# Paged attention with its score rows standing twice on the partitions

## The chip, the cores and the metric

One core of one Trainium2 chip runs the whole program in one launch. The metric is the device time of one execution in microseconds (us). Three runs of the kernel before gave 2151.07, 2154.58 and 2155.91 us, a median of 2154.58 us.

## The reference

One layer of a decoder is computed for a prompt (1 x 1024 tokens) and for samples (8 sequences of 8 new tokens), with the same weights. The change touches only the attention of the samples, which have 2048 cached tokens each, kept in pages of 128:

```
past_c  = cache_kv_latent[l][page_table].reshape(8, 2048, 256)
past_pe = cache_k_rope[l][page_table].reshape(8, 2048, 32)
c_keys  = concatenate([past_c, c_new]);  pe_keys = concatenate([past_pe, pe_new])
s  = (einsum('bqhl,btl->bhqt', q_lat, c_keys) + einsum('bqhr,btr->bhqt', q_pe, pe_keys)) * ATTN_SCALE
s  = where(query position >= key position, s, -1e30)
pr = softmax(s)                                   # float32, 8 heads x 8 queries = 64 rows, 2048 + 8 keys
o  = einsum('bhqt,btl->bqhl', pr, c_keys)
```

The convolution group of the same layer, a causal depthwise convolution of width 31 over 4 x 128 channels, also matters: its taps run on VectorE inside this stage.

## The kernel before, in words

The program is a row of stages, each with one instruction stream per engine, written out by hand with counting semaphores; no scheduler moves anything. The stage here is `paged_attention_stage`; a stage begins when all engines have left the one ahead. It takes the 8 sequences b = 0 to 7 one after the other (a loop over six of them, two written out behind it).

For one sequence the 64 rows R (8 heads x 8 queries) stand on partitions 0 to 63. GpSimd gathers the pages (`gather_pages`, two indirect DMAs, 2 MB and 256 KB, into one of two buffers); for sequence b+2 it waits on `attended` of sequence b, since that frees the buffer. TensorE runs, in this order for step b:

- `turn(b+1)`: 36 transposes of gathered tiles in nine groups q = 0 to 8, through two PSUM banks in turn. ScalarE copies groups 0, 1, 2, 7 and 8 out (`ACT_GROUPS`), VectorE 3 to 6 (`DVE_GROUPS`, L1354); group q waits until group q-2 is copied.
- `attend(b)`: when `exped` says that the exponentials are there, 16 transposes of the probabilities (L1245) and one of the new tokens' (L1249); when they have been copied to SBUF (L1343, L1404), 16 products with the gathered latents (L1255, 64 columns loaded, 256 streamed) and one with the new tokens (L1257).
- `score(b+1)`: for each of four blocks of 512 keys one product with the rope keys (L1223) and two with the latents (L1225), 64 columns loaded and 512 streamed; then three for the 64 new tokens (L1228, L1230). Behind the second block stands `turn_out(b)` (L1263), which transposes the output and waits on `normed`, VectorE's scaled output.

VectorE, for each step: mask on the new tokens' scores (L1385), maximum over 2048 scores (L1387) and over the new (L1389), their joint maximum times the scale (L1391); the four copies of `turn`; sum and reciprocal (L1396, L1398); copies of the turned probabilities (L1403, L1404); then about twelve taps of the convolution, each one instruction on 128 x 1024 (L378) and one on 128 x 64 (L381), split 5:4:2 by the scaling of the output (L1408) and the copy of the turned output (L1412). ScalarE stages the queries of b+1 (L1310, L1312), copies, and takes the exponentials (L1334, L1336).

A float32 product is one instruction of the program and two records in the trace; a transpose is one record.

Of the kernel before, what the change touches and what calls it, by code (L numbers as in the profile page):

```python
# [18 lines left out]
P = 128  # L19
# [1053 lines left out]
def paged_attention_stage(nc, K):  # L1073


    with ExitStack() as ctx:
# [13 lines left out]
        def taps_at(b, part):  # L1090
# [12 lines left out]
        prob = sb("prob", [R, PAST + SAMPLE])  # L1103
        prob_t = sb("prob_t", [P, PER_ROW * R])
        prob_new = sb("prob_new", [SAMPLE, R])
        o = sb("o", [R, KV_LORA])
        tops, sums = sb("tops", [R, 3]), sb("sums", [R, 4])
# [15 lines left out]
            sem(x) for x in ("new_masked", "tops_found", "top_ready", "exped", "summed", "inv_ready"))  # L1123
        probs_turned, act_probs, dve_probs, attended, normed, o_turned, o_copied, may_go = (
# [3 lines left out]
        scores = K.ps[0:R, 0:BANK, :].rearrange("p a b -> p (a b)")  # L1128
        prob_banks = [K.ps[:, 6, :], K.ps[:, 5, :]]
        last = K.ps[:, 7, :]  # L1130
        o_acc, s_new = last[0:R, 0:KV_LORA], last[0:R, 256:256 + SAMPLE]
# [6 lines left out]
        def token(position):  # L1138


            own, j = divmod(position, BANK)
            return j * BANK + own
# [28 lines left out]
        def _(pe):  # L1171
# [44 lines left out]
            def score(b, between=None):  # L1216

                copied(b, GROUPS)
                copied(b, GROUPS - 2)
                pe.wait_ge(staged, 2 * b + 2)  # L1220
                for c in range(BANK):
                    at = slice(c * 512, (c + 1) * 512)
                    nc.tensor.matmul(scores[:, at], q_rope[:, c * R:(c + 1) * R], rope_t[:, :], start=True, stop=False)  # L1223
                    for l in range(KC):
                        nc.tensor.matmul(scores[:, at], q_lat[:, l, :], lat_t[:, l, at], start=False, stop=l == KC - 1)  # L1225
                    if c == 1 and between is not None:
                        between()
                nc.tensor.matmul(s_new, q_rope[:, 2 * R:3 * R], new_rope_t[:, :], start=True, stop=False)  # L1228
                for l in range(KC):
                    mm = nc.tensor.matmul(s_new, q_lat[:, l, :], K.c[:, l, SEQ:T], start=False, stop=l == KC - 1)  # L1230
                mm.then_inc(scored, 1)

            def attend(b, s, more):
                pe.wait_ge(exped, 2 * b + 2)
                if more:

                    copied(b + 1, GROUPS - 1)

                pe.wait_ge(o_copied, KC * b)

                pe.sem_inc(may_go, 1)
                for h in range(2):
                    for j in range(PER_ROW // 2):
                        t = h * (PER_ROW // 2) + j
                        mm = nc.tensor.transpose(prob_banks[h][:, j * R:(j + 1) * R], prob[:, t * P:(t + 1) * P],  # L1245
                                                 K.ident[0:R, 0:R])
                    if h == 0:
                        mm.then_inc(probs_turned, 1)
                nc.tensor.transpose(new_turn, prob[:, PAST:], K.ident[0:R, 0:R]).then_inc(probs_turned, 1)  # L1249
# [7 lines left out]
                nc.tensor.matmul(o_acc, prob_new[:, :], new_rows[:, :], start=False, stop=True).then_inc(attended, 1)  # L1257

            def turn_out(b):
                pe.wait_ge(normed, b + 1)  # L1260
                pe.sem_inc(may_go, 1)
                for l in range(KC):
                    mm = nc.tensor.transpose(o_turn[:, l * R:(l + 1) * R], o[:, l * P:(l + 1) * P],  # L1263
                                             K.ident[0:R, 0:R])
                mm.then_inc(o_turned, 1)
# [8 lines left out]
            pe.wait_ge(prepared, 5)  # L1274
            pe.wait_ge(lat_out, 2)
# [19 lines left out]
        def _(act):  # L1295
# [10 lines left out]
            def stage(b):  # L1306

                if not isinstance(b, int) or b > 0:
                    act.wait_ge(scored, b)
# [17 lines left out]
            def step(b, s, more):  # L1327
                if more:
                    stage(b + 1)
                    copies(b + 1, ACT_GROUPS[0:3])  # L1330
                act.wait_ge(top_ready, b + 1)
# [4 lines left out]
                nc.scalar.activation(prob[:, PAST:], s_new, ACT.Exp, bias=tops[:, 2:3], scale=SCALE,  # L1336
                                     accum_out=sums[:, 1:2]).then_inc(exped, 1)
# [4 lines left out]
                act.wait_ge(attended, b)  # L1342
# [5 lines left out]
        def _(dve):  # L1348
            def copies(b):
                if b > 0:  # L1350
                    dve.wait_ge(scored, b)
# [6 lines left out]
            nc.vector.memset(new_rope_t[:, :], 0.0).then_inc(prepared, 1)  # L1358
            dve.wait_ge(rows_turned, 1)
# [23 lines left out]
            def step(b, s, more):  # L1383
                dve.wait_ge(scored, b + 1)
# [4 lines left out]
                nc.vector.tensor_reduce(tops[:, 1:2], s_new, AX_X, ALU.max).then_inc(tops_found, 1)  # L1389
                dve.wait_ge(tops_found, 2 * b + 2)  # L1390
                nc.vector.tensor_scalar(tops[:, 2:3], tops[:, 0:1], tops[:, 1:2], -SCALE, ALU.max, ALU.mult  # L1391
                                        ).then_inc(top_ready, 1)
                if more:
                    copies(b + 1)
                dve.wait_ge(exped, 2 * b + 2)
                nc.vector.tensor_tensor(sums[:, 2:3], sums[:, 0:1], sums[:, 1:2], ALU.add).then_inc(summed, 1)  # L1396
                dve.wait_ge(summed, b + 1)
                nc.vector.reciprocal(sums[:, 3:4], sums[:, 2:3]).then_inc(inv_ready, 1)  # L1398
                dve.wait_ge(probs_turned, 2 * b + 2)

                if b > 0:
                    dve.wait_ge(attended, b)
# [3 lines left out]
                dve.wait_ge(inv_ready, b + 1)  # L1406
                dve.wait_ge(attended, b + 1)
                nc.vector.tensor_scalar(o[:, :], o_acc, sums[:, 3:4], None, ALU.mult).then_inc(normed, 1)  # L1408
# [1344 lines left out]
```

## Time and profile before

| | |
|---|---|
| median of three runs | 2154.58 us |
| the profiled execution | 2156.27 us |
| its span, first to last instruction | 2154.40 us |
| busy, of the span: TensorE (PE) / VectorE (DVE) / ScalarE (ACT) / GpSimd (POOL) | 90% / 56% / 22% / 24% |
| paged stage: first score product / last tap | 221.99 us / 448.19 us |
| in it, from the first mask (235.75) to the last (425.11): 189.36 us, busy PE / DVE | 178.37 / 164.36 us |

Busy time of an engine is the union of its records. PEld is the loading of weights, which runs beside PE. Matmul records overlap, so the distance of two starts, and not the length of a record, is what one costs in a stream. The granted clock of TensorE is 1.00 at 2.4 GHz and 0.50 at 1.2 GHz.

### The profile page before, as it was taken

The page shows a single profiled execution, that of the slowest core. Times are in us where ns is not written, and L with a number is a line of the kernel's source. Part 1 is how long each engine was busy: PE and PEld are TensorE (multiplying, and loading weights), DVE is VectorE, ACT ScalarE, POOL GpSimd, SP SyncE. Part 2 cuts the span into 40 slices and gives each one's busy share as a digit, 9 for nine tenths or more (in the row PEclk, how much of TensorE's full clock was granted, in tenths as well). Part 3 has the DMA queues.
Part 4 walks back from the last instruction along what each step waited for, and adds up shares of the span by engine and source line. Part 5 has one row for each costly group of instructions (what it writes and reads, how often), then busy time and mean ns, then how long its engine had stood idle before and what let it go on. Part 6 is the DMA issues. An engine that isn't in the chain of part 4 may idle for free. (4 is left out here: it accounts for less than half of the span.)

```text
span 2154.4 us, 27922 instructions
## 1 busy us (share of the span) xinstructions
PE 1941.5 (90%) x10946; PEld 1696.6 (79%) x10946; DVE 1195.8 (56%) x1720; ACT 479.4 (22%) x789; POOL 517.5 (24%) x277
## 2 busy tenths in 40 slices
PE   6998999889999898799948979999999999999985
PEld 6997444445667897689827968999999999999984
DVE  7785588856756437723313578454445445444537
ACT  4021222124444523212212233001001101100011
POOL 3330011010000127821003532322322323223220
PEclk9999999989999999899979989999999999999997
DMA  5215222110000213400072211111111111111102
GB/s 161 84 40 86 88 88 88 44 59 1 1 1 1 90 41 110 146 33 18 0 285 99 77 52 40 40 49 39 39 49 39 41 46 39 49 39 39 49 14 83
DMA packets 42712, 128.37 MB, mean 60 GB/s; under 512 B 12464, under 2 KB 18736, under 8 KB 40016
## 3 DMA queue, kind: packets, MB, share of 16 engines
q1 hardware_dynamic: 40128, 105.72, 14.7%
q0 software_dynamic: 1792, 18.88, 2.3%
q10 hardware_dynamic: 720, 2.79, 0.4%
q8 instruction: 49, 0.80, 0.2%
q14 instruction: 23, 0.19, 0.0%
HBM read 118.81 MB, written 8.56 MB: 59 GB/s over the span
## 5 line engine op out<-in xcount | busy, mean ns | idle before, releaser
L252 POOL CAST w_hi<-raw 128x1024 fp32r<-128x1024 f32 x114 | 136.2, 1195 | 1184.6 <-PE ps L281 621.2
L281 PE MATMUL ps<-xo_hi,w_hi 128*128 128x384 f32 (+1 forms) x1248 | 295.3, 335 | 36.9 <-DVE xo L2458 16.3
L254 POOL TENSOR_TENSOR w_lo<-raw,w_hi 128x1024 fp32r<-128x1024 f32 x114 | 300.8, 2638 | 9.1
L281 PE MATMUL ps<-xo_lo,w_hi 128*128 128x384 f32 (+1 forms) x1248 | 291.5, 331 | 0.0
L281 PE MATMUL ps<-xo_hi,w_lo 128*128 128x384 f32 (+1 forms) x1248 | 291.0, 331 | 0.0
L281 PEld LDWEIGHTS ps<-xo_hi,w_hi 128*128 128x128 f32 x1248 | 219.3, 190 | 43.8 <-issue 35.9
L281 PEld LDWEIGHTS ps<-xo_lo,w_hi 128*128 128x128 f32 x1248 | 219.7, 190 | 0.2
L281 PEld LDWEIGHTS ps<-xo_hi,w_lo 128*128 128x128 f32 x1248 | 219.1, 190 | 0.0
L2413 DVE TENSOR_TENSOR ffn_g_prompt<-ffn_g_prompt,ffn_rstd 128x1024 f32<-128x1024 f32 x22 | 67.8, 3082 | 208.8 <-ACT ffn_g_sample L2293 208.8
L2458 DVE TENSOR_TENSOR xo<-ps,xo 128x768 f32<-128x768 f32 (+1 forms) x160 | 108.4, 719 | 134.1 <-PE ps L281 134.1
L378 DVE SCALAR_TENSOR_TENSOR x<-u_prompt,vecs,x 128x1024 f32<-128x1024 f32 x120 | 163.1, 1359 | 0.0
L281 PE MATMUL ps<-ffn_hid_hi,w_hi 128*128 128x384 f32 (+2 forms) x528 | 130.3, 345 | 8.4 <-DVE ffn_hid_lo L2450 4.8
L281 PE MATMUL ps<-ffn_hid_lo,w_hi 128*128 128x384 f32 (+2 forms) x528 | 123.6, 332 | 0.0
L281 PE MATMUL ps<-ffn_hid_hi,w_lo 128*128 128x384 f32 (+2 forms) x528 | 122.8, 331 | 0.0
L281 PE MATMUL ps<-hx_hi,w_hi 128*128 128x384 f32 (+1 forms) x384 | 90.8, 345 | 14.9 <-PEq L1429 8.4
L281 PEld LDWEIGHTS ps<-ffn_hid_hi,w_hi 128*128 128x128 f32 x528 | 91.7, 191 | 14.8 <-issue 8.8
L281 PEld LDWEIGHTS ps<-ffn_hid_lo,w_hi 128*128 128x128 f32 x528 | 92.4, 191 | 3.4 <-issue 3.0
L871 PEld LDWEIGHTS ps<-v,mla_prob_t 128*128 128x128 f32 x576 | 72.7, 191 | 27.8 <-issue 23.4
L281 PEld LDWEIGHTS ps<-ffn_hid_hi,w_lo 128*128 128x128 f32 x528 | 92.1, 191 | 0.7
L281 PE MATMUL ps<-h_hi,w_hi 128*128 128x384 f32 x336 | 77.1, 338 | 17.1 <-DVE h_lo L614 17.1
L2302 ACT ACTIVATE ffn_hid_hi<-ffn_hid 128x1088 fp32r<-128x1088 f32 x22 | 24.5, 1112 | 294.3 <-PE ps L281 259.2
L281 PE MATMUL ps<-hx_lo,w_hi 128*128 128x384 f32 (+1 forms) x384 | 86.2, 333 | 0.0
(326 smaller groups left out, 3281.9 us busy)
## 6 DMA issues: line engine op xcount, KB each, us to landing
raw<-in_units SPq DMA_DIRECT2D x128, 512.0 KB, 3.2
xs_keys<-in_cache_k_t SPq DMA_DIRECT2D x8, 1024.0 KB, 10.0
xs_vals<-in_cache_v_t SPq DMA_DIRECT2D x16, 512.0 KB, 12.7
x<-in_x_t SPq DMA_DIRECT2D x8, 544.0 KB, 9.0
out_y_t<-x SPq DMA_DIRECT2D x2, 1792.0 KB, 6.6
out_old<-in_x_t ACTq DMA_DIRECT2D x5, 544.0 KB, 3.7
out_old<-in_x_t SPq DMA_DIRECT2D x3, 544.0 KB, 7.0
mla_wq<-in_w_q_t SPq DMA_DIRECT2D x1, 1536.0 KB, 9.0
```

The source lines that it names most:

```text
L252: nc.gpsimd.tensor_copy(K.w_hi[:, s, :], K.raw[:, s, :]).then_inc(K.hi_done[s], 1)
L254: nc.gpsimd.tensor_tensor(K.w_lo[:, s, :], K.raw[:, s, :], K.w_hi[:, s, :].bitcast(F32), ALU.subtract).then_inc(K.split_done[s], 1)
L281: mm = nc.tensor.matmul(out(at, n), w, x(k, at, n), start=first and k == 0 and p == 0, stop=last and k == len(tiles) - 1 and p == 2)
L378: nc.vector.scalar_tensor_tensor(cv, u, scale, cv, ALU.mult, ALU.add).then_inc(tapped, 1)
L871: mm = nc.tensor.matmul(o_acc, prob_t[:, n % 2 * QT + j, :], K.v[:, j, h, :], start=j == 0, stop=j == i)
L2302: nc.scalar.activation(hid_hi[:, slot, :], hid[:, :], ACT.Identity).then_inc(hid_hi_made, 1)
L2413: nc.vector.tensor_tensor(g_p, g_p, rstd[:, 0:SEQ], ALU.mult).then_inc(g_scaled, 1)
L2458: ins = nc.vector.tensor_tensor(y_at, acc, y_at, ALU.add)
```

## The change

The 64 rows stand twice on the partitions: partitions 0 to 63 (`LOWER`) hold the first 1024 keys of the past, 64 to 127 (`UPPER`) the second. Score blocks c and c+2 go to the two halves of the same PSUM bank, and their products alternate; the same for the 16 products of L1255, of which t goes to the lower and t+8 to the upper half of `o_acc`. The past's scores are then 128 x 1024, and maximum, exponential and the copy of the output work on 128 partitions. VectorE joins the two halves' maxima and sums by copies from one half to the other. The probabilities take eight transposes of 128 x 128 in place of sixteen of 64 x 128. The two halves of the output are added in `turn_out`, which becomes a product with `fold` (two identities above one another, made once). `turn_out` now stands behind the first pair of blocks. `scored`, `attended`, `top_ready`, `inv_ready`, `tops_found` and `summed` count more steps each; two semaphores are added, one of them not used.

```diff
-        scores = K.ps[0:R, 0:BANK, :].rearrange("p a b -> p (a b)")
+        LOWER, UPPER = slice(0, R), slice(R, 2 * R)
+        scores = K.ps[:, 0:BANK // 2, :].rearrange("p a b -> p (a b)")
...
-                    pool.wait_ge(attended, b - 1)
+                    pool.wait_ge(attended, 2 * b - 2)
...
-                for c in range(BANK):
-                    at = slice(c * 512, (c + 1) * 512)
-                    nc.tensor.matmul(scores[:, at], q_rope[:, c * R:(c + 1) * R], rope_t[:, :], start=True, stop=False)
+                for c in range(BANK // 2):
+                    halves = [(rows, c + BANK // 2 * n) for n, rows in enumerate((LOWER, UPPER))]
+                    for rows, d in halves:
+                        nc.tensor.matmul(K.ps[rows, c, :], q_rope[:, d * R:(d + 1) * R], rope_t[:, :], start=True,
+                                         stop=False)
                     for l in range(KC):
-                        nc.tensor.matmul(scores[:, at], q_lat[:, l, :], lat_t[:, l, at], start=False, stop=l == KC - 1)
-                    if c == 1 and between is not None:
+                        for rows, d in halves:
+                            mm = nc.tensor.matmul(K.ps[rows, c, :], q_lat[:, l, :], lat_t[:, l, d * 512:(d + 1) * 512],
+                                                  start=False, stop=l == KC - 1)
+                    if c == 0 and between is not None:
                         between()
+                mm.then_inc(scored, 1)
...
-                for t in range(PER_ROW):
-                    if t == PER_ROW // 2:
+                for t in range(2 * BANK):
+                    if t == BANK:
                         pe.wait_ge(dve_probs, b + 1)
-                    at = token(t) * KV_LORA
-                    nc.tensor.matmul(o_acc, prob_t[:, t * R:(t + 1) * R], past[s][:, at:at + KV_LORA], start=t == 0,
-                                     stop=False)
+                    for n, rows in enumerate((LOWER, UPPER)):
+                        at = token(t + 2 * BANK * n) * KV_LORA
+                        mm = nc.tensor.matmul(o_acc[rows], prob_t[:, t * P + n * R:t * P + (n + 1) * R],
+                                              past[s][:, at:at + KV_LORA], start=t == 0, stop=n == 1 and t == 2 * BANK - 1)
+                mm.then_inc(attended, 1)
...
-                    mm = nc.tensor.transpose(o_turn[:, l * R:(l + 1) * R], o[:, l * P:(l + 1) * P],
-                                             K.ident[0:R, 0:R])
+                    mm = nc.tensor.matmul(o_turn[:, l * R:(l + 1) * R], o[:, l * P:(l + 1) * P], fold[:, :],
+                                          start=True, stop=True)
...
-                nc.scalar.activation(prob[:, 0:PAST], scores, ACT.Exp, bias=tops[:, 2:3], scale=SCALE,
+                nc.scalar.activation(prob[:, :], scores, ACT.Exp, bias=tops[:, 3:4], scale=SCALE,
                                      accum_out=sums[:, 0:1]).then_inc(exped, 1)
...
+            nc.vector.tensor_tensor(fold[:, :], K.ident[:, 0:R], K.ident[:, R:2 * R], ALU.add).then_inc(folded, 1)
...
                 nc.vector.tensor_reduce(tops[:, 0:1], scores, AX_X, ALU.max).then_inc(tops_found, 1)
...
+                nc.vector.tensor_copy(tops[LOWER, 2:3], tops[UPPER, 0:1]).then_inc(tops_found, 1)
+                dve.wait_ge(tops_found, 4 * b + 3)
+                nc.vector.tensor_tensor(tops[LOWER, 2:3], tops[LOWER, 2:3], tops[LOWER, 1:2], ALU.max
+                                        ).then_inc(tops_found, 1)
...
+                dve.wait_ge(top_ready, 2 * b + 1)
+                nc.vector.tensor_copy(tops[UPPER, 3:4], tops[LOWER, 3:4]).then_inc(top_ready, 1)
...
-                nc.vector.tensor_scalar(o[:, :], o_acc, sums[:, 3:4], None, ALU.mult).then_inc(normed, 1)
+                nc.vector.tensor_scalar(o[:, :], o_acc, sums[:, 4:5], None, ALU.mult).then_inc(normed, 1)
```

On TensorE, from the transposed probabilities of one sequence to `turn_out` in the score of the next, before (`paged_prob` are the probabilities, `paged_prob_t` their transposes, `x` a buffer of gathered latents, `v` the transposed latents):

```order
L1245 MATMUL ps<-ident,paged_prob 128x64 x16
L1249 MATMUL ps<-ident,paged_prob 64x64
L1255 MATMUL ps<-x,paged_prob_t 64x256 x16
L1257 MATMUL ps<-paged_new_rows,paged_prob_new 64x256
L1174 REGISTER_ALU
L1220 ISA
L1223 MATMUL ps<-paged_rope_t,paged_q_rope 64x512
L1225 MATMUL ps<-v,paged_q_lat 64x512 x2
L1223 MATMUL ps<-paged_rope_t,paged_q_rope 64x512
L1225 MATMUL ps<-v,paged_q_lat 64x512 x2
L1263 MATMUL ps<-ident,paged_o 128x64 x2
```

and the same place now:

```order
L1259 MATMUL ps<-ident,paged_prob 128x128 x8
L1263 MATMUL ps<-ident,paged_prob_tail 64x64
L1270 MATMUL ps<-x,paged_prob_t 64x256 x16
L1273 MATMUL ps<-paged_new_rows,paged_prob_new 64x256
L1182 REGISTER_ALU
L1228 ISA
L1232 MATMUL ps<-paged_rope_t,paged_q_rope 64x512 x2
L1236 MATMUL ps<-v,paged_q_lat 64x512 x4
L1279 MATMUL ps<-paged_fold,paged_o 128x64 x2
```

The number of score and output products and their shapes stay; their order changes, so that neighbours write different halves of the partitions, and eight transposes go. `turn_out` stands behind the same number of products, and has become a product.

On VectorE, from the maximum over the scores to the reciprocal of the sum, before (`paged_tops` holds maxima, `paged_sums` sums; `v<-ps` are the four copies of `turn`):

```order
L1387 TENSOR_REDUCE paged_tops<-ps 64x1
L1389 TENSOR_REDUCE paged_tops<-ps 64x1
L1391 TENSOR_SCALAR paged_tops<-paged_tops 64x1
L1354 COPY v<-ps 128x2x256 x4
L1396 TENSOR_TENSOR paged_sums<-paged_sums 64x1
L1398 RECIPROCAL paged_sums<-paged_sums 64x1
```

and now:

```order
L1405 TENSOR_REDUCE paged_tops<-ps 128x1
L1407 TENSOR_REDUCE paged_tops<-ps 64x1
L1409 COPY paged_tops<-paged_tops 64x1
L1411 TENSOR_TENSOR paged_tops<-paged_tops 64x1
L1414 TENSOR_SCALAR paged_tops<-paged_tops 64x1
L1417 COPY paged_tops<-paged_tops 64x1
L1371 COPY v<-ps 128x2x256 x4
L1421 COPY paged_sums<-paged_sums 64x1
L1423 TENSOR_TENSOR paged_sums<-paged_sums 64x1
L1425 TENSOR_TENSOR paged_sums<-paged_sums 64x1
L1427 RECIPROCAL paged_sums<-paged_sums 64x1
L1429 COPY paged_sums<-paged_sums 64x1
```

Three one-column instructions are added ahead of the four copies and three behind them.

## Rows read from the trace of the kernel before

**Rows 1.** Windows: length, busy us (records) of PE, PEld, DVE, ACT, POOL, clock, DMA.

```profile
222.00:227.65 5.65, 5.65 (x7) 1.63 (x8) 0.00 (x0) 0.00 (x0) 0.58 (x1) 0.50 0.97 376
227.65:235.75 8.10, 8.10 (x26) 2.88 (x25) 0.00 (x1) 0.00 (x0) 0.00 (x0) 1.00 0.07 29
263.36:289.97 26.61, 25.46 (x120) 13.20 (x121) 23.70 (x40) 6.32 (x12) 3.41 (x2) 1.00 0.23 89
289.97:317.65 27.68, 25.55 (x120) 13.19 (x121) 23.49 (x39) 7.49 (x13) 3.41 (x2) 1.00 0.23 85
425.11:429.05 3.94, 0.00 (x0) 0.00 (x0) 2.75 (x4) 1.12 (x1) 0.00 (x0) 1.00 0.00 0
429.05:435.88 6.83, 5.46 (x26) 3.75 (x27) 3.69 (x8) 1.82 (x5) 0.00 (x0) 0.50 0.00 0
```

**Rows 2.** Timeline, sequence 1: start, length, engine, line, what, [idle before, releaser].

```profile
263.37 0.22 DVE L1385 TENSOR_TENSOR ps<-ps,paged_mask 64x64 f32<-64x64 f32 x1 [2.05 <-PE ps L1230]
...
265.94 0.20 DVE L1391 TENSOR_SCALAR paged_tops<-paged_tops 64x1 f32<-64x1 f32 x1
...
266.07 2.71 DVE L1354 COPY v<-ps 128x512 f32<-128x512 f32 x4
...
270.94 0.22 DVE L1403 COPY paged_prob_new<-ps 64x64 f32<-64x64 f32 x1 [1.91 <-PE ps L1249]
...
278.66 1.07 PE L1223 MATMUL ps<-paged_rope_t,paged_q_rope 128*64 128x512 f32 x2
278.84 0.47 DVE L1408 TENSOR_SCALAR paged_o<-ps,paged_sums 64x256 f32<-64x256 f32 x1
...
287.70 1.88 PE L1225 MATMUL ps<-v,paged_q_lat 128*64 128x512 f32 x4
...
289.97 0.23 DVE L1385 TENSOR_TENSOR ps<-ps,paged_mask 64x64 f32<-64x64 f32 x1 [0.65 <-PE ps L1230]
290.04 1.28 ACT L1310 ACT_TABLE_LOAD   x1 [19.06 <-PE ps L1230]
...
293.74 2.92 DVE L1354 COPY v<-ps 128x512 f32<-128x512 f32 x4 [0.98 <-PE ps L1213]
```

**Rows 3.** Groups of instructions in the paged stage: busy us, mean ns, idle before.

```profile
L1225 PE MATMUL ps<-v,paged_q_lat 128*64 128x512 f32 x128 | 61.9, 607 | 0.0
L1255 PE MATMUL ps<-paged_past,paged_prob_t 128*64 128x256 f32 x128 | 30.2, 396 | 0.4
L1387 DVE TENSOR_REDUCE paged_tops<-ps 64x1 f32<-64x2048 f32 x8 | 18.2, 2273 | 0.0
L1334 ACT ACTIVATE paged_prob<-ps,paged_tops 64x2048 f32<-64x2048 f32 x8 | 15.7, 1960 | 23.2 <-DVE paged_tops L1391 23.2
```

**Rows 4.** Timeline of TensorE in the sample cross-attention stage, four 32-row outputs alternating.

```profile
1137.44 3.64 PE L1962 MATMUL ps<-xs_vals,xs_prob_t 128*32 128x512 f32 x32 [0.52 <-DVE xs_prob_t L2017]
```

**Rows 5.** Timeline of the last gather DMAs of sequences 1 and 2, and their median landing.

```profile
221.63 0.95 POOL L688 DMA_INDIRECT past_rope<-in_cache_pe,page_rows  x1 [0.30 <-issue]
...
252.40 2.33 POOL L688 DMA_INDIRECT x<-in_cache_c,page_rows  x1 [29.82 <-PE ps L1257]
...
255.03 1.09 POOL L688 DMA_INDIRECT past_rope<-in_cache_pe,page_rows  x1 [0.30 <-issue]
...
past_rope<-in_cache_pe,page_rows POOLq DMA_INDIRECT x7, 7.8
```

**Rows 6.** Weight loads of eight transposes, at the half clock and at the full.

```profile
203.19 1.57 PEld L1213 LDWEIGHTS ps<-ident,x 128*128 128x128 f32 x8 [0.23 <-ACT paged_rope_t L1300]
...
264.61 0.91 PEld L1213 LDWEIGHTS ps<-ident,x 128*128 128x128 f32 x8 [0.49 <-ACT paged_rope_t L1300]
```

**Rows 7.** Timeline of TensorE in the last sequence.

```profile
430.42 1.94 PE L1245 MATMUL ps<-ident,paged_prob 64*128 64x64 f32 x16 [5.35 <-ACT paged_prob L1336]
...
432.39 8.82 PE L1255 MATMUL ps<-paged_past,paged_prob_t 128*64 128x256 f32 x32
...
441.14 0.64 PE L1257 MATMUL ps<-paged_new_rows,paged_prob_new 64*64 64x256 f32 x2
```

More of the change, by code:

```diff
@@ L1102, in paged_attention_stage @@
         mask = sb("mask", [R, DEC_B * SAMPLE])
-        prob = sb("prob", [R, PAST + SAMPLE])
+        prob = sb("prob", [P, PAST // 2])
+        prob_tail = sb("prob_tail", [R, SAMPLE])
         prob_t = sb("prob_t", [P, PER_ROW * R])
         prob_new = sb("prob_new", [SAMPLE, R])
-        o = sb("o", [R, KV_LORA])
-        tops, sums = sb("tops", [R, 3]), sb("sums", [R, 4])
+        o = sb("o", [P, KV_LORA])
+        fold = sb("fold", [P, R])
+        tops, sums = sb("tops", [P, 4]), sb("sums", [P, 5])
         qlat = sb("qlat", [P, KC * DEC_B, R])[:, :, :].rearrange("p (l b) r -> p l b r", l=KC)
@@ L1127, in paged_attention_stage @@
         block = ctx.enter_context(nc.Block())
-        scores = K.ps[0:R, 0:BANK, :].rearrange("p a b -> p (a b)")
+        LOWER, UPPER = slice(0, R), slice(R, 2 * R)
+        scores = K.ps[:, 0:BANK // 2, :].rearrange("p a b -> p (a b)")
         prob_banks = [K.ps[:, 6, :], K.ps[:, 5, :]]
         last = K.ps[:, 7, :]
-        o_acc, s_new = last[0:R, 0:KV_LORA], last[0:R, 256:256 + SAMPLE]
+        o_acc, s_new = last[:, 0:KV_LORA], last[LOWER, 256:256 + SAMPLE]
         new_turn, o_turn = K.ps[0:SAMPLE, 0, 0:R], K.ps[:, 6, 0:KC * R]
@@ L1242, in attend @@
                 for h in range(2):
-                    for j in range(PER_ROW // 2):
-                        t = h * (PER_ROW // 2) + j
-                        mm = nc.tensor.transpose(prob_banks[h][:, j * R:(j + 1) * R], prob[:, t * P:(t + 1) * P],
-                                                 K.ident[0:R, 0:R])
+                    for j in range(BANK):
+                        t = h * BANK + j
+                        mm = nc.tensor.transpose(prob_banks[h][:, j * P:(j + 1) * P], prob[:, t * P:(t + 1) * P],
+                                                 K.ident[:, :])
                     if h == 0:
                         mm.then_inc(probs_turned, 1)
-                nc.tensor.transpose(new_turn, prob[:, PAST:], K.ident[0:R, 0:R]).then_inc(probs_turned, 1)
+                nc.tensor.transpose(new_turn, prob_tail[:, :], K.ident[0:R, 0:R]).then_inc(probs_turned, 1)
                 pe.wait_ge(act_probs, b + 1)
-                for t in range(PER_ROW):
-                    if t == PER_ROW // 2:
+                for t in range(2 * BANK):
+                    if t == BANK:
                         pe.wait_ge(dve_probs, b + 1)
-                    at = token(t) * KV_LORA
-                    nc.tensor.matmul(o_acc, prob_t[:, t * R:(t + 1) * R], past[s][:, at:at + KV_LORA], start=t == 0,
-                                     stop=False)
-                nc.tensor.matmul(o_acc, prob_new[:, :], new_rows[:, :], start=False, stop=True).then_inc(attended, 1)
+                    for n, rows in enumerate((LOWER, UPPER)):
[3 more added lines that the diff above has]
+                mm.then_inc(attended, 1)
+                nc.tensor.matmul(o_acc[LOWER], prob_new[:, :], new_rows[:, :], start=False, stop=True).then_inc(attended, 1)
             def turn_out(b):
@@ L1274, in _ @@
             pe.wait_ge(prepared, 5)
+            pe.wait_ge(folded, 1)
             pe.wait_ge(lat_out, 2)
@@ L1308, in stage @@
                 if not isinstance(b, int) or b > 0:
-                    act.wait_ge(scored, b)
+                    act.wait_ge(scored, 2 * b)
                 nc.scalar.activation(q_lat[:, :, :], qlat[:, :, bass.ds(b, 1), :].rearrange("p l a r -> p l (a r)"),
@@ L1350, in copies @@
                 if b > 0:
-                    dve.wait_ge(scored, b)
+                    dve.wait_ge(scored, 2 * b)
                 for q in DVE_GROUPS:
@@ L1383, in step @@
             def step(b, s, more):
-                dve.wait_ge(scored, b + 1)
+                dve.wait_ge(scored, 2 * b + 2)
                 nc.vector.tensor_tensor(s_new, s_new, mask[:, b * SAMPLE:(b + 1) * SAMPLE], ALU.add
```

35 lines of the change are left out of this document (21 added, 14 removed).

## The prediction

> **What bounds the kernel now.** I read the page first (TensorE busy 90% of the span, VectorE 56%), then the windows of the paged stage, since a share over the span says nothing of one stage, then the timeline of one sequence there. The windows make both engines look like the bound: in sequence 1, of 26.61 us TensorE is busy 25.46 and VectorE 23.70 [rows 1]. The timeline says how they stand to each other. The reader is to see three points of VectorE: the mask at 263.37, L1403 at 270.94, the next mask at 289.97 [rows 2]. Between the first two VectorE waits for TensorE's transposes (1.91 us at L1403). Behind L1403 it has copies and taps that wait for nothing, until 289.97 - 0.65 = 289.32: 18.4 us. Beside these TensorE does its output and score products, 270.94 to 289.97: 19.0 us. So the part of TensorE that the change shortens runs beside 18.4 us of VectorE which it does not shorten, and VectorE waits only 0.65 us for it (2.05 us in the first sequence, the wait at 263.37).
>
> **TensorE's products.** In a stream of 512 columns a record costs 0.43 us: four take 1.88, less the last one's length of about 0.6, over three [rows 2, 3]. A score over the past has 12 products, 24 records, 10.3 us; the 32 output records fill 278.66 - 270.94 less 0.7 for L1257 and the start, 7.0 us [rows 2]. No row of before has two 64-row halves alternating. The nearest is the sample cross attention, where four 32-row outputs alternate: 32 records of 512 columns in 3.64 us, against 32 x 0.43 = 13.8 one after the other [rows 4]. They run almost four beside one another, at the same spacing. Bounds: nothing gained (each alone) to half the time; I take half, 5.2 us of the score and 3.5 of the output, 8.7 a sequence, some 70 us of TensorE's time in eight. Eight big transposes for sixteen small ones I cost at nothing (twice the columns, half the number), between 0.5 us gained and lost, and `fold` at 0.1 us of TensorE, hidden by its own new slack; without that slack they would be in full on the path. The Trainium skill, "TensorEngine Tiling (Array Packing)", "Tiling Modes", says that changing the tiling mode drains TensorE. No row shows the price here; taking the length of a record over its spacing, 0.16 us, three times a sequence, it would be 0.5 us of the same slack and 0.5 us of the sum at the end.
>
> **VectorE, sequences 1 to 6.** Four of their steps take 26.6 us and two, where ScalarE loads a table ahead of its copies, 27.68 (one of each in [rows 1]): 161.8 us. Now: the maximum reads half as many scores per partition, 2.27 us [rows 3] becomes 1.2; three one-column steps come ahead of the copies, 0.20 to 0.24 each as L1391 [rows 2], +0.7. The three behind the copies fall into the 1.9 us at L1403 and cost nothing; with that wait gone they would cost 0.7. With the 0.65 gone, a step is 26.6 - 0.65 - 1.1 + 0.7 = 25.6 us at TensorE's full clock. In the other two the copies start 293.74 - 289.97 = 3.8 us behind the mask instead of 2.7; `scored` will now come before the mask, so that the table load (1.28 us [rows 2]) is over in time, and these too are 25.6. Gain: 161.8 - 6 x 25.6 = 8.2 us.
>
> **What is late next.** Count from L1403. The output products end at +4.3, and only then may the next gather start. It takes 0.3 + 2.6 us of issue and 7.8 to land, 10.7 in all (252.40 to 255.03 and on [rows 5]): +15.0. The score's first half is done at +7.0, waits for the scaled output (278.84 + 0.47 - 270.94 = +8.4 [rows 2]) and ends at +12.5. So the gather, hidden today behind 11 us of score, will hold TensorE from +12.5 to +15.0; then three groups of `turn` go through, and TensorE waits again for VectorE's first copy, which stands behind its taps and maximum: +18.4 + 2.6 + 0.7 = +21.7. None of this delays VectorE, but TensorE now idles about 10 us of 25.6 in pieces of 2 to 4 us. After 3.94 us without a record its clock was 0.50 for 6.83 us, 5.46 of them busy [rows 1]. I expect that fall in most steps, just before groups 5 to 8 of `turn` and the transposes of the probabilities, and these are on VectorE's path. Weight loads of eight transposes take 1.57 us at half clock and 0.91 at full [rows 6], 0.08 us a record; 25 records are 2.1 us, of which the copies between groups hide a part. Bounds 0 and 2.1 a step; I take 1.2, or 7.2 us in six, so that 1.0 us of the 8.2 is left. The Trainium skill, "TensorE: Matmul & The Clock Gate", "HAM oscillation", says that bursts between waits run at half clock, which is against this change; by it alone the price would be the full 2.1 a step.
>
> **Head.** The first score runs from 222.00 to the mask at 235.75 with nothing else to do, 5.65 us of it at half clock [rows 1]. Twelve pairs and one of stagger: 6.6 at 0.86 us in these 5.65, 6.4 at 0.43 = 2.8, then 0.65 for the new tokens: 9.1 instead of 13.75. Gain 4.65. The gather of sequence 1 has landed at 221.63 + 7.8 = 229.4 [rows 5], before 231.1. The wait of 2.05 us behind it, in the first step, goes as well.
>
> **Tail.** In the last sequence nothing stands beside: maximum -0.4, exponential (1.96 us [rows 3] to about 1.1) -0.9. From the first transpose to the end of L1257 is 430.42 to 441.78, 11.4 us [rows 7]. With 5.46 us at half clock as before: nine transposes 2.0, eight pairs at 0.43, eight at 0.22, 0.65: 7.8. At half clock throughout 10.2. Gain 4.9, at least 2.5; I take 4.4.
>
> **Sum.** 4.65 + 2.05 + 1.0 + 4.4 = 12.1 us off the profiled execution's 2156.27, 2144.2; the median of the runs stands 1.7 below that execution, so 2142.5. With every bound at its worse end 4.65 + 2.05 + 8.2 - 12.6 + 2.5 = 4.8 off, 2149.8.
>
> **Rivals.**
> (a) The clock holds, or its fall lies in VectorE's shadow: 4.65 + 2.05 + 8.2 + 4.9 = 19.8 off, 2134.8. For it: in the step with the table load TensorE has 27.68 - 25.55 = 2.1 us without a record, and the clock stays at 1.00 [rows 1]. Against: the new waits are longer and come twice a step. 20%.
> (b) The halves do not run beside each other, and the change does not do what it says: 64-row outputs are no 32-row ones. Then 19.0 us beside 18.4 stay, and the rest is within 2 us: 2154.5. Against it [rows 4]. 10%.
> (c) Slower: the half clock lasts through output and score. Output 16 x 0.43 + 1.4 = 8.3, score 12 x 0.86 + 1.9 = 12.2, together 20.5 us: past VectorE's 18.4, from where TensorE decides again, and its transposes follow at half clock, 7.6 + 2.1 = 9.7. Six steps of 30.2 and twice 1.1 for the table load are 183.4, +21.6; +1 in the first step, less 4.65 and 2.5: 15.5 slower, 2170. For it: a clock lost anew each 25 us. Against: it came back after 5.65 us of products at 227.65 and after 5.46 at 435.88 [rows 1], and here some 10 us follow without a pause. 10%.
>
> **Chances.** The forecast 60%, 2136 to 2150. About 0.2%, 4.3 us, is what a measurement tells from no change. Faster: the forecast but for 5 of its 60, and (a): 0.75. Same: those 5 and (b): 0.15. Slower: (c), 0.10. The range from 2133 to 2153 leaves out (c) and the outer part of (a) and (b).
>
> **What the new profile would show.** Right: two records of the score starting within some 0.05 us or overlapping by whole lengths, 24 in about 5.5 us; the mask without a wait for TensorE from sequence 1 on, masks 26 to 27.5 us apart in all steps alike; TensorE idle ahead of the first transposes of each sequence and again ahead of group 5, clock 0.50 at these; the first mask near 231. Wrong: masks 25.6 apart with a clock of 1.00 (a); score records 0.43 apart one by one (b); masks that wait for the score, which runs at 0.86 a pair (c). A VectorE step behind L1403 much over 18.4 us would break the sum in a way that I have not costed.

## The result and the profile after

| | us, median (range, runs) | of the kernel before, ratio [95%] |
|---|---|---|
| before | 2155.39 (2151.07 to 2155.91, 5) | |
| changed | 2145.1 (2138.83 to 2146.33, 5) | 0.9948 [0.9937, 0.9959] |
| changed, once more in the experiments | 2145.57 (2133.01 to 2146.8, 6) | 0.9939 [0.992, 0.9958] |

Faster by 10 us, where 12 were forecast. The profiled execution of the first row took 2138.83 us (span 2137.0), the lowest of its five; that of the second 2146.8 (span 2145.0), the highest of its six and 1.2 above their median. Below, "the first" and "the second" are these two executions; most lines shown are of the first, and the account uses both.

One sequence in the first (timeline from the mask of sequence 1 to that of sequence 2; columns as in [rows 2]):

```profile
252.89 0.22 DVE L1403 TENSOR_TENSOR ps<-ps,paged_mask 64x64 f32<-64x64 f32 x1
253.03 1.21 DVE L1405 TENSOR_REDUCE paged_tops<-ps 128x1 f32<-128x1024 f32 x1
...
255.01 0.15 DVE L1417 COPY paged_tops<-paged_tops 64x1 f32<-64x1 f32 x1
255.19 1.29 DVE L1371 COPY v<-ps 128x512 f32<-128x512 f32 x2
...
255.93 1.25 PE L1221 MATMUL ps<-ident,x 128*128 128x128 f32 x8 [1.86 <-DVE v L1371]
...
258.81 1.06 PE L1259 MATMUL ps<-ident,paged_prob 128*128 128x128 f32 x8 [0.18 <-ACT v L1319]
...
260.08 0.22 DVE L1434 COPY paged_prob_new<-ps 64x64 f32<-64x64 f32 x1 [1.24 <-PE ps L1263]
260.12 3.67 PE L1270 MATMUL ps<-paged_past,paged_prob_t 128*64 128x256 f32 x32
...
264.30 1.08 PE L1232 MATMUL ps<-paged_rope_t,paged_q_rope 128*64 128x512 f32 x4
...
265.21 1.89 PE L1236 MATMUL ps<-v,paged_q_lat 128*64 128x512 f32 x8
266.00 1.09 POOL L688 DMA_INDIRECT past_rope<-in_cache_pe,page_rows  x1 [0.30 <-issue]
267.78 0.47 DVE L1439 TENSOR_SCALAR paged_o<-ps,paged_sums 128x256 f32<-128x256 f32 x1
268.40 0.63 PE L1279 MATMUL ps<-paged_fold,paged_o 128*128 128x64 f32 x4 [1.30 <-DVE paged_o L1439]
268.96 1.08 PE L1232 MATMUL ps<-paged_rope_t,paged_q_rope 128*64 128x512 f32 x4
...
271.70 0.40 PE L1244 MATMUL ps<-c,paged_q_lat 128*64 128x64 f32 x4
...
274.03 0.65 PE L1221 MATMUL ps<-ident,past_rope 128*128 128x128 f32 x4 [1.94 <-DMA past_rope<-in_cache_pe,page_rows]
...
278.18 0.22 DVE L1403 TENSOR_TENSOR ps<-ps,paged_mask 64x64 f32<-64x64 f32 x1
...
281.22 3.07 PE L1221 MATMUL ps<-ident,paged_past 128*128 128x128 f32 x14 [2.93 <-DVE v L1371]
```

The reader is to see four things. Eight records of L1236 take 1.89 us, where four took 1.88 [rows 2]; the 32 of the output take 3.67. The mask has no bracket: nothing kept VectorE waiting. TensorE, done with the score at 272.10, waits 1.94 us for the gather and then 2.93 us for VectorE's first copy. And L1434 still waits 1.24 us for TensorE: but for 0.15 at the copies of `turn` (L1371), the one place in the step where VectorE does.

The groups of the paged stage (busy us, mean ns, idle before), against [rows 3]:

```profile
L1236 PE MATMUL ps<-v,paged_q_lat 128*64 128x512 f32 x128 | 31.5, 613 | 0.0
L1270 PE MATMUL ps<-paged_past,paged_prob_t 128*64 128x256 f32 x128 | 15.9, 404 | 0.2
L1405 DVE TENSOR_REDUCE paged_tops<-ps 128x1 f32<-128x1024 f32 x8 | 9.7, 1209 | 0.0
L1351 ACT ACTIVATE paged_prob<-ps,paged_tops 128x1024 f32<-128x1024 f32 x8 | 8.9, 1114 | 40.4 <-DVE paged_tops L1417 40.4
```

The mean of a product is what it was (613 against 607 ns) and the busy time half (31.5 against 61.9): same products, two at a time.

Windows of head and first steps of the second execution (length, busy us (records) of PE, PEld, DVE, ACT, POOL, clock, DMA, as in [rows 1]):

```profile
223.14:231.62 8.48, 8.45 (x32) 3.25 (x33) 0.00 (x1) 0.00 (x0) 0.62 (x1) 0.68 0.74 278
231.62:256.92 25.30, 20.12 (x133) 11.64 (x132) 22.40 (x44) 8.94 (x18) 2.14 (x2) 1.00 0.25 94
256.92:284.06 27.14, 19.54 (x113) 11.81 (x113) 23.64 (x46) 6.87 (x13) 2.21 (x2) 0.87 0.24 88
284.06:310.76 26.70, 20.38 (x110) 12.76 (x110) 23.19 (x47) 5.70 (x12) 2.34 (x2) 0.81 0.24 89
```

A step in which the clock was granted in full takes 25.30; one with a fall takes up to 27.14, longer than most steps of before. A fall need not cost anything: the step shown from the first, 25.29 us, has a mean clock of 0.90. Cut at the first score, the masks of sequences 0, 1 and 7 and the last tap, the profiled executions give (us):

| stretch | before | changed, first | second | second less before | forecast |
|---|---|---|---|---|---|
| ahead of the first score | 221.96 | 219.66 | 223.14 | +1.2 | 0 |
| head, to the first mask | 13.79 | 7.93 | 8.48 | -5.3 | -4.65 |
| first step | 27.62 | 25.30 | 25.30 | -2.3 | -2.05 |
| steps 1 to 6 | 161.75 | 157.16 | 160.38 | -1.4 | -1.0 |
| tail, to the last tap | 23.08 | 17.88 | 18.25 | -4.8 | -4.4 |
| behind the stage | 1706.2 | 1709.1 | 1709.4 | +3.2 | 0 |

In the second, the four stretches that the sum spoke of give 13.8 us, where 12.1 were forecast, and 4.4 are lost outside them. The part ahead of the stage differs from execution to execution: the change alters next to nothing there, and the first is 2.3 us shorter than before where the second is 1.2 longer. Behind the stage, beginning 21 us after its last tap, the clock is 0.50 for 10.2 us in both executions of the changed kernel and for 6.8 us in that of before.

### The profile page after: what moved, and what is told of

It reads as the page before. It is cut to its first block and busy times, and to the rows that moved or that the text cites. A ratio compares the mean times of both kernels' runs of the same rounds, so it can differ in the third digit from the quotient of the medians.

```text
span 2137.0 us, 27883 instructions
## 1 busy us (share of the span) xinstructions
PE 1884.7 (88%) x10898; PEld 1678.8 (79%) x10898; DVE 1194.2 (56%) x1769; ACT 473.8 (22%) x789; POOL 510.1 (24%) x277
## 5 line engine op out<-in xcount | busy, mean ns | idle before, releaser
L2444 DVE TENSOR_TENSOR ffn_g_prompt<-ffn_g_prompt,ffn_rstd 128x1024 f32<-128x1024 f32 x22 | 67.8, 3080 | 208.9 <-ACT ffn_g_sample L2324 208.8
```

The lines of the kernel that those rows point to most:

```text
L2444: nc.vector.tensor_tensor(g_p, g_p, rstd[:, 0:SEQ], ALU.mult).then_inc(g_scaled, 1)
```

## The experiments

**Theory and rivals.** Theory: VectorE's work in its own order sets a step now, so what TensorE saved has become waiting, and the clock that falls in these waits lengthens the transposes that VectorE waits for at L1434. Rivals: TensorE and its clock alone decide (a shorter VectorE would bring nothing); the gather decides; the halves' overlap hangs on the order in which their products are written. Each result is given as median (range, runs) and as a ratio to the kernel before with its 95% interval; traces are of one execution each.

**The change again** (`again`): no edit; its numbers are above.

> The changed kernel once more, nothing edited, so that the part of its time that differs from execution to execution is seen beside its trace. Theory V (VectorE's work in order sets the step; TensorE's freed time became waits): a median of 2143 to 2147 us; masks 25.3 to 27.2 us apart; where a step is over 25.5 us, TensorE's granted clock is 0.50 in groups 5 to 8 of turn and the transposes of the probabilities. Theory C (the low clock decides each step): steps with the clock at 1.00 are several us shorter than 25 us.

As the theory had it: 2145.57 us, masks 25.3 to 27.1 apart, and in each of steps 1 to 6 the clock fell (means of 0.81 to 0.89). The one step at 1.00 takes 25.30, not several us less.

**Not alternating** (`serial`): block by block all products of the lower half, then of the upper.

```diff
                     for rows, d in halves:
                         nc.tensor.matmul(K.ps[rows, c, :], q_rope[:, d * R:(d + 1) * R], rope_t[:, :], start=True,
                                          stop=False)
-                    for l in range(KC):
-                        for rows, d in halves:
+                        for l in range(KC):
...
-                for t in range(2 * BANK):
...
-                    for n, rows in enumerate((LOWER, UPPER)):
+                for n, rows in enumerate((LOWER, UPPER)):
+                    for t in range(2 * BANK):
```

> The layout on 128 partitions stays, but the products do not alternate: in each score block the three of the lower half come first, then the three of the upper, and in the output the eight lower ones before the eight upper. Instructions and their number are the same. Theory V: TensorE needs about 19 us again from L1434's counterpart to the next mask, beside VectorE's 18.4, the clock stays at 1.00, masks are 26.2 to 27.6 us apart, head and tail lose 4 to 6 us together: 2150 to 2156 us. Rival L (the gain comes from the maximum and the exponential on 128 partitions, not from alternating): 2145 us, unchanged.

2139.61 us (2137.78 to 2143.26, 5), 0.9927 [0.9914, 0.994]: a miss, faster than the theory and the rival had it. TensorE in its sequence 1:

```profile
263.85 6.31 PE L1269 MATMUL ps<-paged_past,paged_prob_t 128*64 128x256 f32 x32
270.09 0.64 PE L1272 MATMUL ps<-paged_new_rows,paged_prob_new 64*64 64x256 f32 x2
270.67 1.07 PE L1232 MATMUL ps<-paged_rope_t,paged_q_rope 128*64 128x512 f32 x2
271.57 0.59 PE L1235 MATMUL ps<-v,paged_q_lat 128*64 128x512 f32 x1
271.58 0.64 PE L1232 MATMUL ps<-paged_rope_t,paged_q_rope 128*64 128x512 f32 x1
272.00 0.59 PE L1235 MATMUL ps<-v,paged_q_lat 128*64 128x512 f32 x1
272.06 0.59 PE L1232 MATMUL ps<-paged_rope_t,paged_q_rope 128*64 128x512 f32 x1
...
278.00 0.59 PE L1235 MATMUL ps<-v,paged_q_lat 128*64 128x512 f32 x1
```

At 271.58 the upper half's first product (L1232) runs beside a record of the lower half (L1235), with three more of the lower's still to come: products of the other half start ahead of some that stand before them. So part of the overlap comes by itself: from the copy that is L1434 in the change (here at 263.81) to the end of the score (278.59, the last line) is 14.8 us, against 12.0 alternating and 19.0 before. TensorE stays busy for 150.7 of the 176.23 us between the first and the last mask (134.95 of 185.67 in the second), its clock falls once in them, and the seven steps take 24.8 to 25.3. The totals' intervals overlap those of the change. Against the second, the steps are 9.4 us shorter and the tail, where the overlap is on the path, 3.0 longer (21.21). In the steps full overlap is worth nothing over this part of it.

**Halves apart** (`apart`): all score products of the lower half, `turn_out`, then all of the upper; in the output the lower, its new token, the upper.

```diff
-                for c in range(BANK // 2):
-                    halves = [(rows, c + BANK // 2 * n) for n, rows in enumerate((LOWER, UPPER))]
+                for n, rows in enumerate((LOWER, UPPER)):
+                    for c in range(BANK // 2):
+                        d = c + BANK // 2 * n
...
-                    if c == 0 and between is not None:
+                    if n == 0 and between is not None:
...
+                    if n == 0:
+                        nc.tensor.matmul(o_acc[LOWER], prob_new[:, :], new_rows[:, :], start=False, stop=True
+                                         ).then_inc(attended, 1)
```

> The layout of the change with its products farther apart: all six of the score's lower half, then turn_out, then all six of the upper; the output's eight lower ones and the new tokens', then the eight upper. In the run named serial, products of the upper half started beside the last three or four records of the lower, so that it did not take the overlap away. Here only those few records can overlap: output 6.3 us, score 10.3 us. Theory V: TensorE needs 18.8 us from the copies of the turned probabilities to the next mask, just past VectorE's 18.1; it does not idle and its clock stays at 1.00; steps of 26.0 us and, with the table load, 27.1; head and tail lose 5 to 7 us: 2147 to 2153 us. Rival L (the gain is that of the maximum and exponential on 128 partitions): steps of 25.3 us, 2140 us.

2149.68 (2141.48 to 2151.72, 8), 0.9972 [0.9961, 0.9983]. The output takes 7.84 us, the score ends (285.66, the last line below) 18.1 us behind the copy at 267.56 that is L1434 in the change, and a step takes 25.5 to 27.6. By the medians about half of the gain is left without the overlap. By the trace, the way from the first to the last mask is 184.04 us, between the two of the change (182.46 and 185.67), whose clock falls there, while that of `apart` does so in one step only. What the change as it ran has over `apart` lies in head and tail: 11.08 and 20.75 us, together 5.1 to 6.0 more than in the change. Here too a product of the next stage, of the lower half, starts (274.42) ahead of the last ones of the upper half's output (275.06):

```profile
274.42 0.64 PE L1232 MATMUL ps<-paged_rope_t,paged_q_rope 128*64 128x512 f32 x1
274.63 0.60 PE L1269 MATMUL ps<-paged_past,paged_prob_t 128*64 128x256 f32 x2
...
275.06 0.38 PE L1269 MATMUL ps<-paged_past,paged_prob_t 128*64 128x256 f32 x1
...
284.21 1.45 PE L1235 MATMUL ps<-v,paged_q_lat 128*64 128x512 f32 x3
```

**Products in the waits** (`fill`): TensorE does products that nobody reads, two in its wait for the gather and four in that for VectorE's first copy, from sequence 1 on; its loop is written out for that.

```diff
+            def fill(n):
+                for _ in range(n):
+                    nc.tensor.matmul(K.ps[:, 2, :], K.ident[:, :], K.qn[:, 0, 0:512], start=True, stop=True)
...
+                    if q == 5:
+                        fill(filled)
...
+                    if b > 0:
+                        fill(2)
                     pe.wait_ge(gathered[1 - s], 16 * (b + s) + 32)
...
-                    turn(b + 1, 1 - s)
+                    turn(b + 1, 1 - s, 4 if b > 0 else 0)
```

> TensorE is kept at work while it waits: from sequence 2 on, two products of the identity with 512 columns ahead of the wait for the gather and four ahead of group 5 of turn, into a bank that nothing reads; TensorE's loop over sequences is written out. Their results are not used. Theory V: the clock stays at 1.00 through sequences 2 to 7, masks are 25.3 us apart (25.3 is the undisturbed step), 4 to 6 us are gained on the changed kernel's median, 2139 to 2142 us. Theory C: steps of 22 to 23 us, 2120 to 2130 us. If the added products end later than the wait, each step loses that (0 to 1 us).

2128.99 (2127.3 to 2132.79, 4), 0.9881 [0.9866, 0.9895]: 16.6 us below the change, where 4 to 6 were expected. The total is one that the rival gave (2120 to 2130), but not by its steps of 22 to 23 us. Two stretches of its trace, a step and the place behind the stage (each 15 us of it, beginning 19.46 us after the last tap), and that place in the change's second execution:

```profile
306.14:331.38 25.24, 23.10 (x128) 12.25 (x127) 23.55 (x47) 6.87 (x13) 2.14 (x2) 1.00 0.25 94
443.25:458.25 15.00, 14.02 (x56) 7.96 (x54) 7.58 (x13) 5.51 (x10) 0.55 (x1) 1.00 0.00 1
```

```profile
455.00:470.00 15.00, 13.80 (x46) 9.93 (x47) 2.50 (x3) 4.29 (x7) 0.00 (x0) 0.66 0.00 0
```

In the step TensorE is busy 23.10 us and does not slow VectorE; the clock is 1.00, and six of seven steps take 24.8 to 25.3, the other 26.1. Of the 19.5 us by which its profiled execution is shorter than the second, 9.1 lie between the first and the last mask, 1.1 in the tail, 1.0 in the head and 7.7 behind the stage, where it shows no fall and the change 10.2 us of it. The fall shows in one pair of lines, prompt attention's 32 products of L808 there (the second, then `fill`):

```profile
456.20 6.19 PE L808 MATMUL ps<-olat,wuv 128*128 128x64 f32 x32 [2.41 <-ACT v L908]
```

```profile
442.26 3.79 PE L808 MATMUL ps<-olat,wuv 128*128 128x64 f32 x32 [0.77 <-ACT v L908]
```

**The loop written out alone** (`unroll`).

```diff
-            sequences(step)(pe)
+            for b in range(DEC_B):
+                step(b, b % 2, b < DEC_B - 1)
```

> The changed kernel with TensorE's loop over sequences written out and nothing added: the part of the runs named fill and tapfill that is not the added products. Theory V: nothing to gain, the clock falls in each sequence as before, masks 25.3 to 27.2 us apart: 2142 to 2147 us. Rival (the written-out loop was what those runs gained): 2129 to 2135 us.

2143.14 (2138.84 to 2144.88, 5), 0.9938 [0.9924, 0.9951], steps of 25.2 to 27.1: what the change does. The step that stands beside the one shown of `fill`:

```profile
310.53:336.68 26.15, 20.47 (x118) 12.52 (x117) 23.63 (x46) 7.28 (x14) 2.13 (x2) 0.83 0.25 91
```

So the written-out loop gains nothing by itself. Against this trace, which differs from `fill` by the products alone, `fill` is 6.2 us shorter from the first to the last mask (176.59 for 182.77) and 7.5 behind the stage.

**A tap in VectorE's wait** (`tap`): one of the taps behind L1434 goes ahead of it, into the idle time there (1.24 us in the lines above).

```diff
+                early = taps_at(b, 0) + (1 if more else 0)
+                conv_taps(nc, K, dve, tapped, FRONT_TAPS, taps_at(b, 0), early)
                 dve.wait_ge(probs_turned, 2 * b + 2)
...
-                conv_taps(nc, K, dve, tapped, FRONT_TAPS, taps_at(b, 0), taps_at(b, 1))
+                conv_taps(nc, K, dve, tapped, FRONT_TAPS, early, taps_at(b, 1))
```

> One tap of the convolution (1.39 us, two instructions) of each of the first seven sequences moves from behind the copies of the turned probabilities to ahead of them, where VectorE waits 1.2 to 2.4 us for TensorE's transposes. The number of instructions is the same. Theory V: a step is shorter by nearly the tap, 1.2 to 1.4 us, seven times: 8 to 10 us off, 2135 to 2138 us. Rival G (the gather, late behind a shorter score, sets the step): no change, 2145 us. Theory C: no change or slower by up to 3 us, since the output products start 0.2 us later.

2132.47 (2127.97 to 2132.99, 4), 0.9892 [0.9877, 0.9906], below the 2135 to 2138 expected; steps of 23.6 to 24.4. One of them:

```profile
302.96:327.02 24.06, 19.12 (x119) 11.44 (x118) 23.53 (x46) 7.23 (x15) 2.32 (x2) 0.93 0.26 98
```

TensorE has the same work, and the steps are up to 2.7 us shorter than in the first: VectorE's order was the bound. The clock still falls (0.93 here, 0.90 to 0.94 in steps 1 to 6), yet the step is not longer for it: with a tap in the wait at L1434, VectorE does not wait for the transposes there.

**Both** (`tapfill`): `tap` and `fill`, with three and two products.

> Both edits together: one tap of each sequence in VectorE's wait ahead of the copies of the turned probabilities, and products that nothing reads in TensorE's waits (three of 512 columns ahead of the gather's landing, two ahead of group 5, from sequence 2 on; TensorE's loop written out). Theory V: the tap's 1.2 us a step and the held clock add up: masks 23.9 to 24.2 us apart, clock 1.00 in sequences 2 to 7, 4 to 8 us below the better of the two alone: 2121 to 2127 us. Theory C (the clock alone): no better than fill, 2129 us.

2126.61 (2125.62 to 2127.64, 4), 0.9868 [0.9853, 0.9882]. A step:

```profile
303.00:327.00 24.00, 22.60 (x129) 12.13 (x129) 23.48 (x46) 7.04 (x14) 2.36 (x2) 1.00 0.26 99
```

VectorE is busy 23.48 of 24.00 us: the step is VectorE's work and no more. The median is in the range expected, but 2.4 us below `fill`, where 4 to 8 were expected, and the intervals overlap. The two gains do not add up in the steps: from the first to the last mask this trace takes 168.40 us and that of `tap` alone 168.53. Holding the clock is worth nothing more once the tap stands in the wait. From the first score to the last tap the traces take 226.2 us (before), 208.3 and 212.4 (the change, first and second), 208.8 (`unroll`), 201.2 (`fill`), 194.4 (`tap`) and 193.5 (this one). Behind the stage this execution again has 10.2 us at 0.50 and 1709.1 us, so what `fill` won behind the stage is absent here.

**Without the taps** (`notaps_after`, `notaps_before`): in either kernel VectorE's taps of this stage are left out but for the two that start a channel block.

```diff
-                conv_taps(nc, K, dve, tapped, FRONT_TAPS, taps_at(b, 0), taps_at(b, 1))
+                few_taps(taps_at(b, 0), taps_at(b, 1))
...
```

> The changed kernel without the convolution's taps in the paged stage: of 89 taps only the two that start a channel block remain, so the convolution's result is left out. VectorE's 18.1 us behind the copies of the turned probabilities fall to about 2. Theory V: VectorE no longer sets the step; the gather does (4.3 us to the end of the output products, 9.7 to its landing, 7.6 for turn and transposes, up to 2 for a low clock): masks 21.7 to 23.7 us apart, TensorE's wait for the gather stays, its wait for VectorE's first copy goes; 20 to 30 us off the steps and 5 off the tail: 2110 to 2122 us. Rival T (TensorE's own products and clock set the step in the changed kernel): masks stay 25.3 to 27 us apart, only the tail's 5 us go, 2140 us.

> The kernel before without the same taps (the convolution's result is left out). Theory V: TensorE's 19.0 us of output and score products stay, so masks stay 26.6 and 27.7 us apart although VectorE is nearly idle; only the tail gains, some 5 us: 2148 to 2152 us. Rival (VectorE already set the step before the change): masks 20 to 24 us apart, 2120 to 2135 us.

The change without taps: 2103.44 (2100.29 to 2104.19, 4), 0.9756 [0.9742, 0.977], 42 us below the change and below the 2110 to 2122 expected; after a first step of 19.3, its steps take 22.0 to 23.5. Before without taps: 2151.2 (2149.76 to 2153.93, 10), 0.9983 [0.9974, 0.9992], 4 us below before, as expected, its steps of 26.6 and 27.7 unchanged. A step of the change and one of before, each without taps:

```profile
295.20:317.60 22.40, 18.64 (x113) 10.94 (x113) 7.27 (x21) 5.57 (x12) 1.89 (x2) 0.92 0.28 105
```

```profile
264.40:291.00 26.60, 25.44 (x120) 13.19 (x121) 7.09 (x15) 6.33 (x12) 1.89 (x2) 1.00 0.24 89
```

With 7 us of VectorE work in both, TensorE fills 25.44 of 26.60 in the one and 18.64 of 22.40 in the other. What holds the changed one at 22 is read from its waits (engine, line, releaser: us in total, times, longest):

```profile
PE ps L1221 <- DMA past_rope<-in_cache_pe,page_rows: 19.0, 7, 3.6
```

In the change itself this wait came to 11.4 us in six. So the gather is next, at some 22 us, and was not what set 25 to 27.

**Two copies to ScalarE** (`acttwo`): `tapfill`, with two of `turn`'s copies moved from VectorE, and the added products from group 5 to group 7.

```diff
-        ACT_GROUPS, DVE_GROUPS = [0, 1, 2, GROUPS - 1, GROUPS], list(range(3, GROUPS - 1))
+        ACT_GROUPS, DVE_GROUPS = [0, 1, 2, 3, 4, GROUPS - 1, GROUPS], list(range(5, GROUPS - 1))
```

> On top of the run named tapfill, two of VectorE's four copies of each turn (groups 3 and 4, 0.69 us each) go to ScalarE, which makes them ahead of the exponentials; the added products move from group 5 to group 7. Theory V: VectorE's step is shorter by what it no longer copies, 1.3 us, to 22.7 us, until the gather (4.3 + 9.7 + 7.6 = 21.7 us at the least) decides: 7 to 10 us off, 2117 to 2121 us. Rival G (the gather decides already at 24 us): 2126 us.

2123.07 (2114.27 to 2127.15, 5), 0.9844 [0.9824, 0.9864]: the fastest of the kernels that do all of the work, though its interval overlaps that of `tapfill`; 2117 to 2121 were expected. Steps 2 to 6 take 22.4 to 23.5, around the 22.7 expected, again full of VectorE:

```profile
352.00:374.80 22.80, 21.27 (x123) 11.52 (x123) 22.22 (x44) 6.56 (x15) 2.14 (x2) 1.00 0.28 105
```

The profiled execution was the fastest of the five, with no fall behind the stage (1701.9 us); no trace of a median run shows why the median is above the expectation.

## Why the prediction was right

**The overlap.** Right: half the time, as [rows 4] let expect of 64-row halves too. 24 score records take 5.6 us (264.30 to 267.10 and 268.96 to 271.76) and 32 of the output 3.67, at the full clock; before, by the same measure, 10.7 and 7.1. That is 8.6 us a sequence, for 8.7 forecast. Rival (b), that the halves do not overlap, fell; `apart`, where next to nothing overlaps, took 2149.7. The drain between tiling modes that the Trainium skill speaks of ("TensorEngine Tiling (Array Packing)", "Tiling Modes") was reckoned at 0.5 us; the lines show no such gap: the last record of L1279, over 128 columns, starts at 268.75 and L1232, over 64, at 268.96, 0.21 us later, where the records of L1279 follow each other at 0.11 to 0.13. That leaves 0.1 us at most at this place.

**VectorE as the bound of a step.** Right, and the point on which the sum stood: taking VectorE's taps away brings 42 us after the change and 4 before it. The size of a step at full clock was 25.6 forecast and 25.28 measured: the mask's wait -0.65, maximum and one-column steps 0.38 less from mask to L1434 (7.19 for 7.57), and 0.29 from L1434 to the next mask (18.09 for 18.38). The last I had called work that waits for nothing; but in before the scaled output at L1408, which needs TensorE's output products, began 1.60 us behind the start of the tap ahead of it, where taps follow each other at 1.39, and now it begins at 1.39: 0.21 of the 0.29 was a wait.

**What is late next.** Right in place: the gather, then VectorE's first copy. TensorE idles 5.8 to 7.7 us in steps 1 to 5, not 10.

**The clock.** The mechanism was right, and rival (a) fell as a forecast of the change: `fill` and `unroll` differ by the products alone, and steps go from 25.2 to 27.1 down to 24.8 to 25.3, with one of 26.1. The price, forecast at 1.2 us a step, was 0.9 in the first profiled execution and 1.4 in the second, over steps 1 to 6, and from 0 to 1.9 in one, so that the steps are not alike, as they were forecast to be. VectorE pays this price at two places, the copies of `turn` and L1434. The transposes of the probabilities take 1.06 us in sequence 1 of the first and 1.94 in the same place of the second:

```profile
261.11 0.69 DVE L1371 COPY v<-ps 128x512 f32<-128x512 f32 x1 [0.61 <-PE ps L1221]
...
263.75 1.94 PE L1259 MATMUL ps<-ident,paged_prob 128*128 128x128 f32 x8
...
265.97 0.22 DVE L1434 COPY paged_prob_new<-ps 64x64 f32<-64x64 f32 x1 [2.39 <-PE ps L1263]
```

There the waits are 0.61 and 2.39 us, for 0.15 and 1.24 in the first. `tap` bears this out: its clock falls too, but with a tap in the wait at L1434 its steps are as long as those of `tapfill` at 1.00. The fall is in each of steps 1 to 6 of both executions (mean clocks of 0.81 to 0.93); its price is not. By the Trainium skill ("TensorE: Matmul & The Clock Gate", "HAM oscillation") alone, by which bursts between waits start at the low clock, the price would have been 2.1 us in each step; the rows agree with it as to the fall, and not as to a price in every step. Rival (c) did not come: the clock was back by the start of the output, which took 3.67 to 3.84 us in steps 1 to 6 of both executions.

**Head and tail.** They gave 5.3 to 5.9 us and 4.8 to 5.2, against 4.65 and 4.4 forecast. In the tail, TensorE from the first transpose to the last output product takes 7.5 us, 413.99 to 421.51, for 11.4 [rows 7]; 7.8 was forecast:

```profile
413.99 1.94 PE L1259 MATMUL ps<-ident,paged_prob 128*128 128x128 f32 x8 [10.02 <-ACT paged_prob_tail L1353]
...
416.10 4.84 PE L1270 MATMUL ps<-paged_past,paged_prob_t 128*64 128x256 f32 x32
...
420.87 0.64 PE L1273 MATMUL ps<-paged_new_rows,paged_prob_new 64*64 64x256 f32 x2
```

**What was missing.** The sum had no term behind the stage, and there 2.9 to 3.2 us were lost, in executions with a longer stretch at half the clock. Across the profiled executions with all the taps the time behind the stage goes with that stretch: none and 1701.5 to 1701.9 (`apart`, `fill`, `acttwo`), 6.8 us and 1706.2 to 1707.2 (before, `serial`), 10.2 us and 1709.1 to 1709.4 (the change twice, `unroll`, `tap`, `tapfill`). What decides among the three is open: `tapfill` and `acttwo` both keep the clock through the steps and differ there, and with one trace each it can be the execution or the edit. That it is the execution is suggested by the runs of `apart` (2141.5, 2142.3 and six of 2149.5 to 2151.7) and of `acttwo` (2114.3, 2114.6 and three of 2123.1 to 2127.2): two groups 7 to 13 us apart, where traces without a fall and with 10.2 us of it differ by some 7.6. But no two executions of either were traced. So of what `fill` gains on the second, the trace shows 11.2 us in head, steps and tail, and the rest stands on this. And that the total came within 2 us of the forecast is in part luck: the four stretches gave 1.7 us more than their terms, and what the sum had no term for took 4.4 away.

## What to carry to other kernels

Before halving an engine's work, find what the other engine does between the same two waits: here 8.6 us of TensorE a sequence bought 1.3 us a step at the full clock, and 0.2 to 0.8 on average as it ran, since 18 us of VectorE stood beside them. Where the saving turns into waits, look at the clock of what follows, and put work of the new bound into its own waits: one tap moved ahead of a wait brought about as much again as the whole change. What stands alone, head and tail, pays in full.

## What the runs showed of the hardware

Products that write the upper 64 rows start ahead of products for the lower rows that stand before them in the program: in `serial` three of the six records of the lower half's score block, and three of the 16 of its output, were still to come when the upper half's first one started. Pairs of the change start 0.007 us apart, and the next pair 0.43 later: the spacing of a single record before.

Six products of 512 columns that nobody reads, in a step of 25 us, made the step shorter: between the first and the last mask TensorE was busy 134.69 of 182.77 us without them (`unroll`) and 151.92 of 176.59 with them (`fill`), at a mean clock of 0.87 and 0.99.

A fall of the clock cost nothing where VectorE did not wait for what it slowed: with a mean clock of 0.93 in the stretch between the first and the last mask, `tap` takes 168.53 us there, and `tapfill`, at 0.99, 168.40.
